# Two-layer hybrid decoder trunk on one core: compression products of the NSA mixer spread between the products of the last projection group, SSD chain one loop step earlier

## The reference

```python
for l in range(DEPTH):                     # DEPTH = 2, 256 tokens, D_MODEL = 1024
    h = rms_norm(h_res, norm_mix[l])
    u = h @ w_in[l]                        # one projection, four groups of columns
    y_a = mla_mixer(u[..., :o1], ...)
    y_b = nsa_mixer(u[..., o1:o2], ...)
    y_c = rglru_mixer(u[..., o2:o3], ...)
    y_d = ssd_mixer(u[..., o3:], ...)
    y = concatenate([rms_norm(y_a), rms_norm(y_b), rms_norm(y_c), y_d])
    h_res = h_res + y @ w_out[l]
    h = rms_norm(h_res, norm_ffn[l])
    h_res = h_res + (swiglu(h) if l % 2 == 0 else moe_ffn(h))   # experts: top 2 of 8
return rms_norm(h_res, norm_final)

# inside nsa_mixer, the part that the change moves: 15 overlapping blocks of 32 tokens, 64 wide
def compress(t, pe, w):
    ch = t.reshape(B, S // 16, 16, 64)
    blk = concatenate([ch[:, :-1], ch[:, 1:]], axis=2)
    return (blk + pe).reshape(B, 15, 32 * 64) @ w
kc, vc = compress(keys, pe[0], w[0]), compress(vals, pe[1], w[1])
```

## Time and profile before

| | us |
|---|---|
| median of 3 runs | 1629.19 |
| lowest, highest | 1625.79, 1631.63 |
| the profiled execution: time | 1629.23 |
| the profiled execution: span of the core | 1627.4 |

### The profile page before, as it was taken

How to read it: one execution, slowest core, us unless ns; L and a number is a source line. 1 busy time by engine, 2 the same in 40 slices (tenths; PEclk the granted TensorE clock), 3 DMA queues, 4 the chain that set the end, 5 groups by cost and what they waited for, 6 DMA issues and landing times.

```text
span 1627.4 us, 20283 instructions
## 1 busy us (share of the span) xinstructions
PE 1546.0 (95%) x7476; PEld 1292.2 (79%) x7476; DVE 1229.1 (76%) x1150; ACT 1017.4 (63%) x941; POOL 81.8 (5%) x110
## 2 busy tenths in 40 slices
PE   7998799999799984999999999999999999999996
PEld 6887688888689864888888888888888888888884
DVE  6747544444567455888989988988988988988985
ACT  5645343444345522778778778778778778777763
POOL 2100000000000001000000000000000000000000
PEclk9968999999898685999999999999999999999998
DMA  9521555555330052999999999999999999999991
GB/s 288 136 61 60 205 187 198 184 181 192 103 118 1 27 181 78 358 395 358 376 394 356 382 393 352 388 393 344 395 394 343 394 396 342 393 397 352 394 397 43
DMA packets 189878, 444.67 MB, mean 273 GB/s; under 512 B 9633, under 2 KB 15918, under 8 KB 189822
## 3 DMA queue, kind: packets, MB, share of 16 engines
q1 hardware_dynamic: 185214, 427.82, 71.6%
q0 software_dynamic: 4608, 16.10, 3.9%
HBM read 436.03 MB, written 7.86 MB: 273 GB/s over the span
## 4 chain that ended last, share of the span: by engine, by line
PE 93%; DVE 3%; issue 2%; ACT 1%; DMA 0%; POOL 0%; SPq 0%; ACTq 0%; DVEq 0%; POOLq 0%
PE bank L451 25%; PE bank L452 25%; PE bank L450 25%; PE bank L578 3%; PE bank L713 2%; PE bank L505 2%; PE bank L679 2%; PE bank L581 1%; PE bank L694 1%; PE bank L731 1%; PE bank L723 1%; DVE hT L1669 1%; PE bank L915 0%; PE bank L430 0%; DVE w_lo L1693 0%
## 5 line engine op out<-in xcount | busy, mean ns | idle before, releaser
L1714 DVE TENSOR_TENSOR w_lo<-ring,w_hi 128x2048 fp32r<-128x2048 f32 x375 | 853.4, 2290 | 193.3 <-ACT w_hi L1281 192.6
L1281 ACT ACTIVATE w_hi<-ring 128x2048 fp32r<-128x2048 f32 x375 | 716.1, 1915 | 221.6 <-PE bank L450 221.5
L451 PE MATMUL bank<-w_hi,xT_hi 128*128 128x512 f32 x896 | 354.4, 396 | 5.8 <-ACT w_hi L1281 5.8
L452 PE MATMUL bank<-w_hi,xT_lo 128*128 128x512 f32 x896 | 350.4, 391 | 0.0
L450 PE MATMUL bank<-w_lo,xT_hi 128*128 128x512 f32 x896 | 240.4, 390 | 0.0
L451 PE MATMUL bank<-w_hi,hidT_hi 128*128 128x512 f32 x560 | 220.5, 394 | 1.6 <-DVE hidT_lo L1721 1.6
L452 PE MATMUL bank<-w_hi,hidT_lo 128*128 128x512 f32 x560 | 218.3, 390 | 0.0
L451 PEld LDWEIGHTS bank<-w_hi,xT_hi 128*128 128x128 f32 x896 | 168.8, 188 | 40.1 <-ACT w_hi L1281 6.2
L450 PEld LDWEIGHTS bank<-w_lo,xT_hi 128*128 128x128 f32 x896 | 168.7, 188 | 35.7
L452 PEld LDWEIGHTS bank<-w_hi,xT_lo 128*128 128x128 f32 x896 | 169.0, 189 | 33.9
L451 PE MATMUL bank<-w_hi,hT_hi 128*128 128x512 f32 (+2 forms) x384 | 150.3, 395 | 7.9 <-DVE hT_lo L1955 4.5
(11 more groups left out here) (344 smaller groups left out, 1380.8 us busy)
## 6 DMA issues: line engine op xcount, KB each, us to landing
ring<-in_moe_w_gate_dram SPq DMA_DIRECT2D x112, 1024.0 KB, 10.0
ring<-in_moe_w_up_dram SPq DMA_DIRECT2D x112, 1024.0 KB, 9.4
ring<-in_moe_w_down_dram SPq DMA_DIRECT2D x112, 1024.0 KB, 9.5
ring<-in_ffn_w_gate_dram SPq DMA_DIRECT2D x14, 1024.0 KB, 5.1
ring<-in_ffn_w_up_dram SPq DMA_DIRECT2D x14, 1024.0 KB, 5.1
ring<-in_ffn_w_down_dram SPq DMA_DIRECT2D x14, 1024.0 KB, 4.8
ring<-in_w_in_dram SPq DMA_DIRECT2D x12, 1024.0 KB, 5.3
ring<-in_w_out_dram SPq DMA_DIRECT2D x8, 1024.0 KB, 5.0
```

The costliest lines, as they stand in the source:

```text
L451: pe.matmul(o, x_hi, w, start=start, stop=False)
L452: return pe.matmul(o, x_lo, w, start=False, stop=False)
L1281: act.activation(w_hi[:, (base + at) % SPLIT, :], ring[:, i, :], ACT.Copy).then_inc(hi_ready, 1)
L1714: dve.tensor_tensor(w_lo[:, v, :], ring[:, (base + at) % RING, :], w_hi[:, v, :].bitcast(F32), ALU.subtract).then_inc(lo_ready, 1)
```

## The change

TensorE: `compressed_keys` and `compressed_values` are replaced by `compress(eighth)`, four products for the keys and four for the values, in turn. `by_channel` calls it after each of the eight groups of the second contraction half of the z projection. The pieces lru_square, ssd_sums, ssd_cb and ssd_products move one step to the front. ACT and DVE follow: the adds that make `cin`, the RG-LRU recurrence and half of the SSD convolution stand ahead of the row maxima of job 0, and the chains of SSD and RG-LRU one step earlier. One semaphore value instead of two says that the compressed keys and values are there.

```diff
+                                if h == 1 and between is not None:
+                                    between(4 * low + i)
...
-                def compressed_keys():
...
-                def compressed_values():
...
+                def compress(eighth):
+
+                    if eighth == 0:
+                        pe.wait_ge(cin_ready, l + 1)
+                        compressed[:] = [bank(0), bank(0)]
+                    keys, values = compressed
+                    for j in range(4 * eighth, 4 * eighth + 4):
+                        last = j == CLEN - 1
+                        mk = pe.matmul(keys[0:HD, 0:NC], w_cmp[0:HD, j, :], cin[0:HD, j, :], start=(j == 0), stop=last)
+                        mv = pe.matmul(values[0:NC, 0:HD], cin[HD:P, j, :], w_cmp[HD:P, j, :], start=(j == 0),
+                                       stop=last)
+                    if eighth == 7:
+                        give(mk, 0, keys)
+                        give(mv, 0, values)
+                        mark["cmp", l] = gave[0]
...
-                by_channel(p + 8, 1, 1, z=True, after={(0, False): turn_qk, (1, False): lambda: scores(0)})
+                by_channel(p + 8, 1, 1, z=True, after={(0, False): turn_qk, (1, False): lambda: scores(0)},
+                           between=compress)
...
-                    if n == 1:
-                        compressed_keys()
                     turn_probs(n - 1, 0 if n == 7 else 1)
                     if n == 2:
-                        compressed_values()
+                        lru_square()
                     if n == 3:
-                        lru_square()
+                        ssd_sums()
                     if n == 4:
-                        ssd_sums()
+                        ssd_cb()
                     if n == 5:
-                        ssd_cb()
-                    if n == 6:
                         ssd_products()
...
+                act.wait_ge(lru_vec, 5 * l + 4)
+                act.activation(lt1[:, :, :], lgate[:, :, :], ACT.Square, scale=GW ** -0.5).then_inc(lru_act, 1)
+
                 for n in range(1, len(AJ)):
                     exps(n)
                     turned_probs(n - 1)
```

107 lines of the change are left out of this document (46 added, 61 removed).

## The result

| | us |
|---|---|
| kernel before, median of 4 runs | 1630.03 (1625.79 to 1631.63) |
| changed kernel, median of 4 runs | 1663.91 (1652.86 to 1668.73) |
| ratio, 95% interval | 1.020 (1.0145 to 1.026) |
| profiled execution of the changed kernel: time, span | 1652.86, 1651.1 |
| forecast, range | 1617, 1601 to 1636 |

The change makes the kernel slower by 34 us, and the forecast of 12 us faster was wrong.

A forecast was written before the change was run, and what follows sets the result against it. PE's own clock, at 0.50 for long mixer stretches, was taken as the bound. Compression -3.5, clock -22.6, new waits +10.4 and a remaining fall +3.4 gave -12.3 us, so 1617 us, range 1601 to 1636.

The forecast's parts named there:

- I take nothing: Compression parts: the 56 turns a layer between key and value products were priced at zero.
- Rival 2: Compression parts: turns drain TensorE at 0.14 us each, clock falls in the high half; 1643 us, chance 0.21.
- Its mark of 0.11 us a turn: Turns between key and value: the price from which rival 2 decides, with the forecast's other terms, 12.3 / 112.
- parts 2 to 4: Mixers: half-clock work returns to full clock, -22.6 us; new PE waits, +10.4; a clock fall that stays, +3.4.
- part 3: Loop after the projection: PE at full clock waits for ACT and DVE, 5.2 us a layer, +10.4 us.
- parts 2 and 4: PE clock in the mixers: -22.6 us from half-clock work at full clock, +3.4 us for a fall that stays.
- part 4: Low half of the projection or just behind: one clock fall a layer, some 7 us, +3.4 us for both layers.
- Rival 1: Compression: keys and values overlap on different rows, 6.1 instead of 9.8 us a layer, clock stays; 1604 us, chance 0.23.
- Rival 3: Mixers: clock falls in the low half and returns only with the running sums; 1627 us, chance 0.14.
- the signs of being wrong: A part over 2 us, clock 0.50 through steps 1 to 3 in both layers, or PE waits over 8 us a layer.

The follow-up runs named there:

- the kernel on 128 rows: Changed kernel with keys and values still in turn, but both on all 128 rows, `cin` kept twice with zeros: 1655.23 us, ratio 1.0149.
- its repair: RG-LRU scaling on DVE moved from step 4 to the end of step 3: 1625.21 us on the changed kernel with four keys then four values, 1643.80 on the changed kernel.
- the grouped kernel: Changed kernel with four keys products, then four values products in each of the eight parts, instead of in turn: 1639.56 us, ratio 1.006.
- the 32 pairs: Kernel before with the compression in step 1 as 32 key and value pairs of one form, one transpose of the values in step 2: 1607.25 us, ratio 0.9865.

## Why the prediction was wrong

**The turn.** The step that failed first is "I take nothing" for the turn from key to value. The row that I chose, transposes with 64 between such with 128 columns, shows no price; a turn between 64 and 15 stationary columns costs 0.10 us. Eight parts cost 8 x 1.70 = 13.6 us a layer instead of 9.8, 7.6 us more in both. The rule of the Trainium skill that I set against the row ("TensorEngine Tiling (Array Packing)", section Tiling Modes) was the right one here, though the row itself doesn't bear it out. I had priced its case at 0.14, from the round trip between 128 and 64 rows, which turned out to be another matter: the turn costs the same on 128 rows throughout.

**The clock in the projection.** Taking from the first stretch what it had without keys before (18.82 - 5.17 and 17.56 - 3.90, 13.7 in each), 27.2 and 19.7 us remain for eight parts. 13.6 of each are the parts at full clock, so the fall of the clock in the projection cost 13.6 and 6.1, together 19.7 us. (The 1.70 leaves out the way into a part and out of it. Against the 28.31 us of the kernel on 128 rows, which has the same turns and full clock, the fall cost 12.6 and 5.1, together 17.7; 2.0 are the way in and out.) The forecast had a fall in the low half or behind it, at 3.4 us for both layers. Rival 2 had this mechanism, parts that outweigh the dense groups and a fall in the high half, at a chance of 0.21. Its mark of 0.11 us a turn counted the turns alone; by that mark a turn of 0.10 would have left the kernel as fast as before. That the clock fell was the larger part of the loss: with one turn a part instead of seven it held through the projection in five of six mixers. At what mixture it falls, no run here shows.

**The loop.** From job 2 to the output projection before has 49.76 and 55.96 us, 91.7 without the values' runs. By parts 2 to 4 of the forecast it was to lose 8.8 us; it lost 0.7 (40.32 + 50.69 = 91.0). These 8.1 us are a net figure. The waits for ACT and DVE were 2.0 us in layer 0 and 4.5 in layer 1, 6.5 instead of the 10.4 of part 3; so the clock gave back 7 us where parts 2 and 4 together had 19. The shortfall lies in layer 1: the clock rises before step 3 as forecast (0.99 from 549 to 557), but falls again at 560 and at 579. The second fall is the one behind the wait for DVE. The forecast did say that DVE would be late in the last steps and had 1.9 us for that; the wait is 1.56. What it left out is that the wait could take the clock with it. The terms add up to the 23.1 us of the table, as each is a measured stretch less its forecast: -12.3 + 7.6 + 19.7 + 8.1 = +23.1. They say where the time went; the causes rest on the experiments. (The 3.4 us of part 4 are counted in the 8.8.)

**The shift.** "The SSD chain one step earlier" stood in no term and no rival by itself; I had looked at the DVE work that moved ahead of the loop, not at which two pieces came to stand in the same step inside it. The runs show it at 11 us, twice, and its repair at 14 and 20.

**What was right.** A grouped part came out near the forecast (1.11 us, and 1.2 with the way in and out: 23.34 less 13.7, over eight), but by luck: eight products at 0.122 are 0.98 and the turn 0.10, so some 0.13 is left for the round trip and not 0.28. Nor is it a matter of rows: on 128 rows throughout the same difference is 0.15. The waits for ScalarE come once PE is fast: 0.77 and 2.18 us in layer 1, though in layer 0 only 0.41, since there the clock came back too late for them; in the grouped kernel, at full clock, they are 1.50 and 1.07 in layer 0 (1.6 and 1.7 forecast). The thin compression products were rightly seen as what stands ahead of the fall, and that less time in them gives clock back; only the means was wrong. Rival 1's overlap is real, and the trace of before could not show that it needs one form. Rival 3 didn't occur: the clock was back by 126 and by 549, ahead of the running sums (131.76 in layer 0), though in layer 1 it was gone again at 560, so that the sums ran at half clock there. Of the signs of being wrong one came: a part took 2.56 us, over 2, once the clock had fallen.

## What to carry to other kernels

Small matmuls that share the array by rows should have the same stationary width: then those on rows 0 to 63 and on rows 64 to 127 run at the same time. It was measured with 64 stationary columns and 15 or 64 moving ones; heads or experts of other sizes are to be measured. Writing the second one transposed and turning it back by one transpose is cheap (with it the kernel gained 22 us of 1630). Before spreading work between dense groups, count the changes of form that the spreading makes: six more a part cost 4.7 us a layer and the clock with them, with one a part the clock held through the projection in five of six traced mixers, and without the shift the time was that of before (ratio 0.9989). And when a chain is moved by one step, list for each engine what then stands together in one step: a wait of 1.5 us on TensorE is cheap only as long as the clock stays.

## What the runs showed of the hardware

- A change of the stationary width from 64 to 15 columns or back, with 64 moving columns on the narrow side, costs 0.10 us each time, on 64 or on 128 rows, while products of one form with 64 rows each on different halves start 0.01 us apart and overlap (eight in 0.57 us, where eight without overlap would be 0.98), even with 15 moving columns on one side and 64 on the other.
- The granted clock fell to 1.2 GHz while PE was busy all the time (85.00 to 125.90 at 0.50) and stayed at 2.4 GHz with a product pace as slow on 128 rows (76.74 to 105.05 at 1.00). In layer 1 the same two kernels fell at the same place, and behind the 32 pairs, which use all rows, it stayed up in layer 0 and fell in layer 1 (0.51), so rows in use are not all of it; and equal work in layers 0 and 1 of one kernel fell 3 us after the first part in one and 16 us after it in the other.
- The stretch from job 4 to the output projection (products of 64 and 15 columns, transposes) was 29.4 to 30.7 us long, at a mean clock of 0.64 to 0.67, in 13 of 14 cases with a wait of 1.56 us in it, and 20.6 to 23.9, at 0.78 to 0.98, in all eight without the wait.
